# Experts' rows added by token block and transposed at once, with the norm scales applied behind the first projections

## The chip, the cores and the metric

The kernel runs on one core of one Trainium2 chip. The metric is the device time of one execution in microseconds (us). The kernel before took 2353.63 us, the median of 3 runs (2353.54 to 2357.41).

## The reference, cut to what matters

Two transformer stacks follow each other on 512 tokens (T) of width 1024 (D). The change lies where the first ends and the second begins:

```python
h = h + hierarchical_moe(rms_norm(h, norm2_g), ...)    # 32 experts, top 2 of each token
x = rms_norm(h, final_g)                                # "final norm" of the first stack
h = x
u = rmsnorm(h, norm_mix[0])                             # "mixer norm" of the second stack
q, f, i, g = split(u @ w_in)                            # hgrn2_mixer, 8 heads of 128
forget = lb + (1 - lb) * sigmoid(f); key = 1 - forget; query = silu(q)
# chunked recurrence over the tokens from key, query, value i and log(forget), out gated by silu(g)
h = h + (o * silu(g)) @ w_out
```

With s the experts' sum of a token, fg the final gain, a = 1/sqrt(mean(s^2)+eps) and b the same root of the vector a\*fg\*s, the residual is a\*fg\*s and the mixer's input is (a\*b)\*(fg\*g_mix\*s). Both a and a\*b are one number for a token.

## The kernel before, in words

**Engines.** PE (TensorE) makes every product and transpose, DVE (VectorE) and ACT (ScalarE) everything elementwise, POOL (GpSimd) some of it and the indirect DMAs, SP (SyncE) issues the weight loads. Each engine runs its own list in order; semaphores tie the lists together.

**Weights in two parts.** Outside the experts every float32 product is three products of rounded parts (`product`, L527 to L531: hi by hi, lo by hi, hi by lo). A weight unit is 128x2048 (1 MB). SP loads it into one of 4 `raw` slots, ACT rounds it to `w_hi` and DVE subtracts to `w_lo` (`split`, L1154 and L1586). Activations are held as `u_hi`, `u_lo`, 8 chunks (KC) of 128 features by 512 tokens.

**Experts.** 17 rounds of 2 experts each. Every round streams 12 units (`moe_w`, L474, L484) and POOL gathers the tokens' rows (L2288) by a slot table that it read back just before (L2282, L2283); the round's results are scattered to `pair_rows` in DRAM (L2298). Behind the last round POOL waits for that scatter, loads `over_slots` (L2307), asks whether any expert overflowed (not here), and issues the four reads of `y_pairs` (L2326), one for each block of 128 tokens.

**Between the stacks.** DVE adds each token's two expert rows to the residual (L1885, L1887, two 128x1024 operations for each block b), ACT squares each row with its sum (L1309), a root and a reciprocal give the final norm's scale, and DVE multiplies the rows by it (`xn`, L1894). Only then does PE transpose them (L810, 32 transposes), and DVE writes the chunks times fg to `hs` (L1899). The mixer norm follows: ACT squares `hs` (L1325), PE sums by a product with ones (L826), ACT takes the root (L1349), DVE the reciprocal (L1906), and for each chunk DVE scales (`u_tmp`, L1915), ACT rounds (`u_hi`, L1358) and DVE subtracts (`u_lo`, L1910).

**Recurrent stage.** 4 pairs of heads (p), each with 4 weight units j: f (j=0), q (j=1), value (j=2), gate (j=3), each in two halves, so 16 "beats" for a pair. The two halves of unit j use PSUM banks (2j+half)%4. ACT reads the PSUM halves itself: Sigmoid (L1439), Silu (L1441), Copy (L1443), Silu (L1446). `recurrent_work(beat)` on each engine does the recurrence's pieces beside the projections, from beat 11 on: POOL forms exponents (`fx`, L2347, L2348), ACT exponentiates them (L1394), DVE multiplies keys (`k_dec`, L2006), POOL queries (`q_dec`, L2360), PE forms scores of a level (L887), DVE takes them by a mask (L2015). Once for each head come the far scores (operands L1376 to L1381 and L1991 to L1995, PE L865 to L871), the head's output (PE L899, DVE L2023) and its norm (PE L908, ACT L1417, DVE reciprocal L2030 and L2031, `o_lo` L2054). f becomes key and log (L2066, L2067, L1429, scan L2075). The order of all this is written by hand:

```python
for half in range(2):               # PE, unit j of pair p
    ... feature_chunk(..., recurrent_work(beat + 2 * half) after its 4th k)
    mm.then_inc(proj_ready if half == 0 else unit_used, 1)
    recurrent_work(beat + 2 * half + 1)
```

Of the kernel before, what the change touches and what calls it, by code (L numbers as in the profile page):

```python
# [7 lines left out]
ALU = mybir.AluOpType  # L8
# [63 lines left out]
def columns(*sizes):  # L72
    at, out = 0, {}
    for name, n in sizes:
# [8 lines left out]
P2_COLS, P2_N = columns(("n2g", D), ("w_r", KC * 36), ("b_r", 36), ("fg", KC), ("pairs", 4 * TB))  # L83
P3_COLS, P3_N = columns(("n_mix", 2 * KC), ("n_ffn", 2 * KC), ("lb", 3 * KC), ("og", 1), ("levels", 8 * P),
                        ("fin", D), ("cos", T), ("sin", T), ("band", 3 * 256))
P3_FIRST = P3_COLS["fin"][0]
P3_ROOM = (P3_FIRST + 7) // 8 * 8
# [28 lines left out]
def build(nc, x_in, weights_in, constants_in, phase1_in, phase2_in, phase3_in, out):  # L116
    with ExitStack() as ctx:
# [11 lines left out]
        at_a = at_par + (max(P1_N, P2_N, P3_N, P3_ROOM + 6 * T) * 4 + 31) // 32 * 32  # L129
# [96 lines left out]
        y_pairs = place("y_pairs", [TB, 2, D], at_a)  # L226
# [20 lines left out]
        u_tmp = [place(f"u_tmp{n}", [T], at_a2 + (3 + n) * KB2) for n in range(3)]  # L247
# [4 lines left out]
        at_room = at_par + P3_ROOM * 4  # L252
# [14 lines left out]
        lbs = [place(f"lbs{n}", [KC], at_x + 384 + 32 * n) for n in range(6)]  # L267

# [101 lines left out]
        def norm_bank(k):  # L370

            return bank[4 if k else 7]

# [39 lines left out]
        y_landed, y_landed_from = [*y_free, table_written, slots_landed], (160, 144, 144, 64)  # L413
# [7 lines left out]
        n_sq, n_sum, n_root, u_ready = sem("n_sq"), sem("n_sum"), sem("n_root"), sem("u_ready")  # L421
# [26 lines left out]
        def _(sp):  # L448
# [38 lines left out]
            for j in range(RAW):  # L487
                sp.wait_ge(unit_used, U_EXTRA + j + 1)
                sp.dma_start(raw[:, j], weights_in[U_EXTRA + j]).then_inc(raw_landed[j], 16)
            def stream(first, end):  # L490
# [30 lines left out]
        def _(pe):  # L521
# [283 lines left out]
            pe.wait_ge(xn_ready, 2 * TB)  # L805
            for c in range(KC):
                if c >= 4:
                    pe.wait_ge(h0_ready, c - 3)
                for b in range(TB):
                    mm = nc.tensor.transpose(bank[c % 4][:, b * P:b * P + P], xn[:, b, c * P:c * P + P], ident)  # L810
                mm.then_inc(h_turned, 1)

            def norm(k):

                at = norm_bank(k)
                if k:
                    pe.wait_ge(n_acc, 6 * k)
                    nc.tensor.matmul(at[:], ones, sq_acc[:], start=True, stop=False)  # L820
# [104 lines left out]
            for p in range(HH // 2):  # L925
                for j in range(4):
# [5 lines left out]
                    if j == 1 and p:  # L932
                        pe.wait_ge(g_taken, 2 * p)
# [1647 lines left out]
```

## Time and profile before

| | |
|---|---|
| median of 3 runs | 2353.63 us |
| the profiled execution, its own time | 2358.84 us |
| its span in the profile | 2357.0 us |
| mean granted TensorE clock | 0.957 |
| busy PE, DVE, ACT, POOL | 88%, 40%, 28%, 15% of the span |

All starts below are microseconds from the span's start. The span holds the first stack's mixer (to about 310), the router and the experts (to 893), the passage between the stacks (893 to 945), the recurrent stage (945 to 1240) and the rest, which the change leaves alone. A start and a duration belong to one instruction or to merged ones (x8 is eight records).

### The profile page before, as it was taken

The numbers are of one execution on the slowest core, as the hardware profiler recorded it, in microseconds if no ns is written. First come the engines' busy times: TensorE is split into PE (matmuls) and PEld (weight loads), VectorE is DVE, ScalarE is ACT, GpSimd is POOL, SyncE is SP. The second block draws the span as 40 slices with busy tenths as digits, with TensorE's granted clock in tenths as the row PEclk, the third lists the DMA queues.
The fourth block names the chain that finished last, engine by engine and source line by source line (L and its number), as shares of the span: only waits on it lengthen the run. The fifth ranks groups of instructions, "written<-read, shape, count | busy, mean of one in ns | idle before, by whom it ended". The sixth has DMA issues, their size and how long they took to land.

```text
span 2357.0 us, 25197 instructions
## 1 busy us (share of the span) xinstructions
PE 2080.2 (88%) x9900; PEld 1510.4 (64%) x9900; DVE 937.3 (40%) x1125; ACT 669.2 (28%) x835; POOL 352.8 (15%) x349
## 2 busy tenths in 40 slices
PE   6997756877777773999989999999999999999997
PEld 5884532332223221788877888887788987888876
DVE  5428640000000004567765432444775334332333
ACT  3433220000000002666744221223222423221222
POOL 0000002000000000355551110011343201100100
PEclk9997777999999997999999999999999999999999
DMA  5220145999999993211122222223222322222220
GB/s 200 90 90 1 51 193 216 422 421 422 421 421 420 421 420 146 72 63 64 57 76 72 90 106 90 90 91 123 76 86 90 138 77 90 90 95 101 89 90 36
DMA packets 57636, 377.51 MB, mean 160 GB/s; under 512 B 8944, under 2 KB 9040, under 8 KB 14032
## 3 DMA queue, kind: packets, MB, share of 16 engines
q1 hardware_dynamic: 50544, 358.83, 38.8%
q0 software_dynamic: 7008, 17.50, 2.0%
q8 instruction: 61, 1.00, 0.2%
q14 instruction: 23, 0.19, 0.0%
HBM read 370.46 MB, written 15.26 MB: 164 GB/s over the span
## 4 chain that ended last, share of the span: by engine, by line
PE 69%; DMA 18%; DVE 7%; issue 3%; ACT 2%; POOL 1%; SPq 0%; DVEq 0%; POOLq 0%; ACTq 0%
PE bank L529 19%; PE bank L530 19%; PE bank L531 19%; DMA moe_w<-weights_in 17%; PE bank L748 2%; PE bank L725 2%; PE bank L887 2%; PE bank L899 1%; POOL k_rot L2398 1%; DVE w_lo L1586 1%; PE bank L1095 1%; DVE tile L1703 1%; DVE o_tmp L2030 0%; DVE tile L1714 0%; DVE tile L1710 0%
## 5 line engine op out<-in xcount | busy, mean ns | idle before, releaser
L529 PE MATMUL bank<-u_hi,w_hi 128*128 128x512 f32 x1216 | 489.0, 402 | 7.6 <-DVE u_lo L1910 6.4
L530 PE MATMUL bank<-u_lo,w_hi 128*128 128x512 f32 x1216 | 481.3, 396 | 0.0
L531 PE MATMUL bank<-u_hi,w_lo 128*128 128x512 f32 x1216 | 481.0, 396 | 0.0
L1586 DVE TENSOR_TENSOR w_lo<-raw,w_hi 128x2048 fp32r<-128x2048 f32 x96 | 234.1, 2439 | 292.8 <-ACT w_hi L1154 292.6
L725 PE MATMUL bank<-moe_w,xe 128*64 128x512 f32 x1088 | 263.3, 632 | 87.7 <-DMA moe_w<-weights_in 86.5
L529 PEld LDWEIGHTS bank<-u_hi,w_hi 128*128 128x128 f32 x1216 | 228.6, 188 | 66.4 <-issue 10.8
L531 PEld LDWEIGHTS bank<-u_hi,w_lo 128*128 128x128 f32 x1216 | 228.5, 188 | 55.9
L530 PEld LDWEIGHTS bank<-u_lo,w_hi 128*128 128x128 f32 x1216 | 228.9, 188 | 55.2 <-issue 2.2
L1154 ACT ACTIVATE w_hi<-raw 128x2048 fp32r<-128x2048 f32 x96 | 183.6, 1912 | 272.1 <-PE bank L531 271.4
L725 PEld LDWEIGHTS bank<-moe_w,xe 128*64 128x64 f32 x1088 | 91.6, 145 | 258.5 <-issue 258.4
L529 PE MATMUL bank<-w_hi,u_hi 128*128 128x256 f32 (+1 forms) x512 | 155.3, 303 | 12.5 <-DVE u_lo L1721 6.8
L530 PE MATMUL bank<-w_lo,u_hi 128*128 128x256 f32 (+1 forms) x512 | 152.7, 298 | 0.0
L531 PE MATMUL bank<-w_hi,u_lo 128*128 128x256 f32 (+1 forms) x512 | 152.4, 298 | 0.0
L1859 DVE TENSOR_TENSOR hid<-gate,bank 128x512 f32<-128x512 f32 x17 | 11.7, 689 | 339.0 <-PE bank L725 339.0
L2387 POOL TENSOR_TENSOR f_gate<-f_gate,rms 128x512 f32<-128x512 f32 x44 | 57.0, 1296 | 566.5 <-ACT f_gate L1471 566.5
L529 PE MATMUL bank<-hid_hi,w_hi 128*128 128x512 f32 x352 | 139.2, 395 | 0.2
L748 PE MATMUL bank<-moe_w,hid_t 128*64 128x512 f32 x544 | 123.6, 596 | 17.7 <-ACT hid_t L1277 6.4
L530 PE MATMUL bank<-hid_lo,w_hi 128*128 128x512 f32 x352 | 139.0, 395 | 0.0
L531 PE MATMUL bank<-hid_hi,w_lo 128*128 128x512 f32 x352 | 139.0, 395 | 0.0
L2103 DVE TENSOR_TENSOR f_hid<-f_gate,bank 128x512 f32<-128x512 f32 x44 | 30.3, 689 | 212.6 <-PE bank L531 212.6
L529 PEld LDWEIGHTS bank<-w_hi,u_hi 128*128 128x128 f32 x512 | 97.7, 191 | 18.1 <-DVE u_lo L1721 8.3
L530 PEld LDWEIGHTS bank<-w_lo,u_hi 128*128 128x128 f32 x512 | 97.7, 191 | 3.1
(395 smaller groups left out, 2645.5 us busy)
## 6 DMA issues: line engine op xcount, KB each, us to landing
moe_w<-weights_in SPq DMA_DIRECT2D x204, 1024.0 KB, 25.1
raw<-weights_in SPq DMA_DIRECT2D x128, 1024.0 KB, 4.8
y_pairs<-pair_rows POOLq DMA_DIRECT2D x4, 1024.0 KB, 8.2
res<-x_in SPq DMA_DIRECT2D x1, 2048.0 KB, 7.7
token_rows<-xn POOLq DMA_DIRECT2D x1, 2048.0 KB, 7.9
v_rows<-vals SPq DMA_DIRECT2D x2, 1024.0 KB
vals<-v_rows SPq DMA_DIRECT2D x2, 1024.0 KB, 7.5
out<-out_tile SPq DMA_DIRECT2D x4, 512.0 KB, 2.6
```

The costliest lines, as they stand in the source:

```text
L529: nc.tensor.matmul(out_ap, a_hi, b_hi, start=first, stop=False)
L530: nc.tensor.matmul(out_ap, a_hi, b_lo, start=False, stop=False)
L531: return nc.tensor.matmul(out_ap, a_lo, b_hi, start=False, stop=last)
L725: mm = nc.tensor.matmul(bank[2 + j // 2][rows, :], xe[:, c, rows], moe_w[2 * j + b][:, w], start=c == 0, stop=c == KC - 1)
L748: mm = nc.tensor.matmul(bank[5 + half][rows, :], hid_t[:, c, rows], moe_w[2 * j + b][:, w], start=c == 0, stop=c == 3)
L887: mm = nc.tensor.matmul(bank[4 + n % 2][:, t], left, right, start=True, stop=True)
L899: mm = nc.tensor.matmul(bank[6][:, b * P:], val[s][:, b, hh * P:hh * P + P], ws[:, b, 0:T - b * P], start=b == 0, stop=b == TB - 1)
L1095: mm = nc.tensor.matmul(bank[6 + i % 2][:, b * P:b * P + P], vals[:, g, from_block, h * P:h * P + P], flat[:, n * P:n * P + P], start=s == ...
L1154: nc.scalar.activation(w_hi[:, n % 2], raw[:, n % RAW], ACT.Copy).then_inc(hi_ready, 1)
L1586: nc.vector.tensor_tensor(w_lo[:, n % 2], raw[:, n % RAW], w_hi[:, n % 2].bitcast(F32), ALU.subtract) \
L2103: nc.vector.tensor_tensor(f_hid[s][:], f_gate[s][:], bank[2 * s + 1][:], ALU.mult).then_inc(f_prod, 1)
L2387: nc.gpsimd.tensor_tensor(f_gate[n][:], f_gate[n][:], rms[:], ALU.mult).then_inc(f_gated, 1)
```

## The change

The two rows of a token are added as before, but into a buffer of their own (`row_sum`), and PE transposes each block's sum as soon as it is there, unscaled. ACT and DVE make `u_hi` and `u_lo` straight from PSUM with the product of both gains, and ACT copies the residual out. The two per-token scales are worked out from row sums beside the first products; two products with ones spread them over all partitions (`spread_late`), and DVE multiplies each projection by them on its way out of PSUM (`normalize`), the value through ACT's scale. POOL multiplies the residual. The `y_pairs` reads move from POOL's queue to SP's; the `over_slots` load moves ahead of the first gather; the second half of the third parameter block is loaded at the start of the router and the lower-bound arithmetic runs there; the Exp for it too.

```diff
 SP, behind the 4 raw loads of the first units, ahead of the raw stream:
+            sp.wait_ge(pairs_stored, PAIRS_STORED)
+            for b in range(TB):
+                sp.dma_start(y_pairs[b][:], pair_rows[...]).then_inc(y_landed[b], 16)
 PE:
-            pe.wait_ge(xn_ready, 2 * TB)
-            for c in range(KC): ...
-                    mm = nc.tensor.transpose(bank[c % 4][...], xn[:, b, ...], ident)
-            norm(0)
+            for b in range(TB):
+                pe.wait_ge(res2_ready, b + 1)
+                for c in range(KC):
+                    mm = nc.tensor.transpose(bank[c][:, b * P:b * P + P], row_sum[:, b, c * P:c * P + P], ident)
+                    if b == TB - 1:
+                        mm.then_inc(h_turned, 1)
+            def spread_late():
+                pe.wait_ge(hs_out, HS_OUT + KC)
+                for n in range(2):
+                    pe.wait_ge(diag_ready, DIAG_READY + n + 1)
+                    nc.tensor.matmul(bank[6 + n][:], ones, late_diag[n][...], start=True, stop=True).then_inc(n_sum, 1)
                     if j == 1 and p:
-                        pe.wait_ge(g_taken, 2 * p)
+                        pe.wait_ge(pre_ready, PRE_READY + 6 * p)
                     if j == 2:
-                        pe.wait_ge(f_sig, 2 * p + 2)
+                        pe.wait_ge(pre_ready, PRE_READY + 6 * p + 2)
                     if j == 3:
-                        pe.wait_ge(q_taken, 2 * p + 2)
+                        pe.wait_ge(pre_ready, PRE_READY + 6 * p + 4)
                     for half in range(2):
+                        if p == 0 and j < 2:
+                            pe.wait_ge(hs_out, HS_OUT + 2 * j + half + 1)
...
+                        if (p, j, half) == (0, 1, 0):
+                            spread_late()
 ACT:
+            def row_square(b): ... ACT.Square, row_sum -> row_sq, accum late[:, 0]
+            def high(c):     # waits h_turned; u_hi from bank[c], scale mix_gain
+            def residual(c): # waits u_lo; hs from bank[c], scale fg
+            for b in range(TB - 1):
+                row_square(b)
+            for c in range(3):
+                high(c)
+            act.wait_ge(res2_ready, TB)
+            residual(0)
+            for c in range(3, KC):
+                high(c)
+            row_square(TB - 1)
+            residual(1)
+            split(U_HG + 1)
+            for c in range(2, KC):
+                residual(c)
+            ... Sqrt of late[:, 4:6]; split(U_HG + 2)
+            ... late_row[0], late_row[1] copied from bank 6, 7
 ACT, each pair (Sigmoid and Silu now from SBUF, behind DVE):
+                            act.wait_ge(pre_ready, PRE_READY + 6 * p + half + 1)
+                            nc.scalar.activation(run[s][:, half], run[s][:, half], ACT.Sigmoid).then_inc(f_sig, 1)
 DVE:
-            ... reciprocal, xn (L1894), hs (L1899), norm(0)
+            for c in range(KC):
+                dve.wait_ge(u_hi_ready, 2 * KC + c + 1)
+                nc.vector.scalar_tensor_tensor(u_lo[:, c], bank[c][:], mix_gain[:, c:c + 1], u_hi[:, c], mult, subtract)
+            row_squares(0); row_squares(1); split(U_HG + 1); row_squares(2); row_squares(3)
+            ... 3 small operations, reciprocal, late_diag[0], late_diag[1], split(U_HG + 2)
+            def normalize(p, j, tile):
+                for half in range(2):
+                    (waits proj_ready or unit_used)
+                    nc.vector.tensor_tensor(tile[:, half], bank[(2 * j + half) % 4][:], late_row[0][:], ALU.mult) \
+                        .then_inc(pre_ready, 1)
                     recurrent_work(beat + 2)
+                    if j == 0 and p:
+                        normalize(p, 0, run[s])
+                    if j == 1:
+                        if p == 0:
+                            dve.wait_ge(late_ready, LATE_READY + 1)
+                            normalize(0, 0, run[s])
+                        normalize(p, 1, qry[s])
+                    if j == 3:
+                        normalize(p, 3, o_raw[:, 2 * p:2 * p + 2])
                     recurrent_work(beat + 3)
 POOL:
+            pool.dma_start(par3[:, P3_FIRST:], phase3_in[:, P3_FIRST:])   # behind par2's, in the router
             pool.wait_ge(slots_landed, 48)
+            pool.dma_start(over_slots[0:CAP], slot_table[MAIN + P:]...).then_inc(slots_landed, 16)
...
-            pool.dma_start(over_slots ...)      # was here, behind the last scatter
             pool.wait_ge(slots_landed, 64)
             (asks for an overflow)
-            for b in range(TB):
-                pool.dma_start(y_pairs[:, b], ...)
+            nc.gpsimd.memset(y_mark[:], 0).then_inc(pairs_stored, 1)
...
+            pool.wait_ge(late_ready, LATE_READY + 2)
+            for c in range(KC):
+                nc.gpsimd.tensor_tensor(hs[:, c], hs[:, c], late_row[1][:], ALU.mult).then_inc(h0_ready, 1)
```

For p = 0 the Ln, the key arithmetic and the Sigmoid stand one unit later than for the other pairs (Sigmoid in j=1, Ln in j=2). The second parameter block grows by 1024 columns (`fg_row`).

## Rows read from the trace of the kernel before

**Rows 1.** The page, the chain that ended last, shares by engine.
```profile
PE 69%; DMA 18%; DVE 7%; issue 3%; ACT 2%; POOL 1%; SPq 0%; DVEq 0%; POOLq 0%; ACTq 0%
```
**Rows 2.** The chain in order of time, 899 to 943: start, duration, what.
```profile
899.08 3.32 DMA over_slots<-slot_table
...
903.89 5.33 DMA y_pairs<-pair_rows
918.12 1.30 DVE res L1887
...
922.35 2.75 DVE xn L1894 x4
925.14 6.13 PE bank L810 x32
931.27 7.46 PE bank L826 x16
...
939.47 3.37 DVE rms L1906
```
**Rows 3.** Timeline of PE, 945 to 983: units j=0, 1, start of j=2, far scores.
```profile
945.14 0.77 PE L529 MATMUL bank<-u_hi,w_hi 128*128 128x512 f32 x1 [6.43 <-DVE u_lo L1910]
...
951.46 0.47 PE L529 MATMUL bank<-u_hi,w_hi 128*128 128x512 f32 x1
...
954.28 0.40 PE L529 MATMUL bank<-u_hi,w_hi 128*128 128x512 f32 x1
...
971.08 0.28 PE L529 MATMUL bank<-w_hi,u_hi 128*128 128x256 f32 x1
...
982.44 0.38 PE L865 MATMUL bank<-far_q,far_k 128*128 128x128 f32 x2
```
**Rows 4.** The windows: busy time of each engine, granted clock, DMA share, GB/s.
```profile
440.00:880.00 440.00, 341.92 (x1518) 129.15 (x1516) 33.64 (x56) 36.62 (x62) 27.45 (x27) 0.96 1.01 421
943.00:950.00 7.00, 4.86 (x12) 3.42 (x12) 6.96 (x12) 3.67 (x6) 0.00 (x0) 0.56 0.00 0
1081.00:1149.00 68.00, 68.00 (x406) 58.36 (x405) 49.11 (x74) 45.06 (x64) 33.91 (x43) 1.00 0.17 63
```
**Rows 5.** Timeline of POOL where the experts begin; SP's first refill.
```profile
368.72 1.05 POOL L2288 DMA_INDIRECT x_rows<-token_rows,slots  x1 [2.17 <-DMA slots<-slot_table]
...
382.12 83.45 SPq L474 DMA_DIRECT2D moe_w<-weights_in  x40
```
**Rows 6.** Single lines (ns: mean, or minimum/median/maximum), and raw's loads to landing.
```profile
L1325 ACT ACTIVATE sq<-hs 128x512 f32<-128x512 f32 x8 | 5.1, 632 | 10.4 <-DVE hs L1899 5.4 <-PE bank L826 4.9
L2103 DVE TENSOR_TENSOR f_hid<-f_gate,bank x44: 689/689/689, 1292.5 to 2282.4; 128x512 f32<-128x512 f32 x44
L2387 POOL TENSOR_TENSOR f_gate<-f_gate,rms x44: 1282/1297/1297, 1290.3 to 2278.2; 128x512 f32<-128x512 f32 x44
DMA to landing us min/median/max: 4.6/4.8/26.1
```
**Rows 7.** Timeline of ACT and DVE beside pair 2's unit j=1, 1099 to 1108.
```profile
1099.72 0.60 ACT L1441 ACTIVATE qry<-bank 128x512 f32<-128x512 f32 x1 [1.57 <-PE bank L531]
1100.34 1.28 ACT L1394 ACT_TABLE_LOAD   x1
...
1101.54 0.42 DVE L2006 TENSOR_TENSOR k_dec<-fx,key 128x256 f32<-128x256 f32 x1
...
1103.70 1.07 DVE L2006 TENSOR_TENSOR k_dec<-fx,key 128x256 f32<-128x256 f32 x1
```
**Rows 8.** Timeline of PE, POOL and DVE, 1103 to 1142, before two level scores.
```profile
1103.26 1.05 PE L887 MATMUL bank<-q_dec,k_dec 128*128 128x128 f32 x8
...
1106.06 2.66 POOL L2347 TENSOR_TENSOR fx<-run 128x256 f32<-128x256 f32 x1
...
1140.57 0.41 DVE L2006 TENSOR_TENSOR k_dec<-fx,key 128x256 f32<-128x256 f32 x1
...
1141.04 1.16 PE L887 MATMUL bank<-q_dec,k_dec 128*128 128x128 f32 x8
```

More of the change, by code:

```diff
@@ L225, in build @@
         over_slots = tiny("over_slots", [N_OVER, 2], I32)
-        y_pairs = place("y_pairs", [TB, 2, D], at_a)
+        y_pairs = [place(f"y_pairs{b}", [2, D], at_b + 20 * KB2 if b == 3 else at_a + 4 * b * KB2) for b in range(TB)]
         MAIN = P * NPAIR
@@ new lines, in _ @@
+                    if j == 1:
+                        for half in range(2):
+                            act.wait_ge(pre_ready, PRE_READY + 6 * p + half + 3)
+                            nc.scalar.activation(qry[s][:, half], qry[s][:, half], ACT.Silu).then_inc(q_taken, 1)
+                    if j == 2:
+                        for half in range(2):
+                            if half == 0:
+                                act.wait_ge(proj_ready, 4 * p + j + 1)
+                            else:
+                                act.wait_ge(unit_used, n + 1)
+                            for b in range(2):
+                                c = slice(b * 256, b * 256 + 256)
+                                last = nc.scalar.activation(val[s][:, 2 * half + b], bank[half][:, c], ACT.Copy,
+                                                            scale=late[:, 7, 2 * half + b:2 * half + b + 1])
+                            last.then_inc(v_taken, 1)
@@ L1447, in _ @@
+                    if j == 3:
+                        for half in range(2):
+                            act.wait_ge(pre_ready, PRE_READY + 6 * p + half + 5)
+                            nc.scalar.activation(o_raw[:, 2 * p + half], o_raw[:, 2 * p + half], ACT.Silu).then_inc(g_taken, 1)
                     recurrent_work(beat + 3)
@@ new lines, in _ @@
+            chain(nc.vector.tensor_scalar(late[:, 3], late[:, 2], EPS, None, ALU.mult))
+            nc.vector.scalar_tensor_tensor(late[:, 3], late[:, 1], 1.0 / D, late[:, 3], ALU.mult, ALU.add).then_inc(rms_arg, 1)
+            dve.wait_ge(root_ready, 4)
+            chain(nc.vector.reciprocal(late[:, 6:8], late[:, 4:6]))
+            for n in range(2):
+                nc.vector.tensor_tensor(late_diag[n][:], ident.unsqueeze(1).to_broadcast([P, TB, P]),
+                                        late[:, 7 - n].unsqueeze(2).to_broadcast([P, TB, P]), ALU.mult).then_inc(diag_ready, 1)
@@ L1920, in split_trip @@
+            split(U_HG + 2)
             def split_trip(n, i, per):
```

228 lines of the change are left out of this document (107 added, 121 removed).

## The prediction

> **What bounds the kernel now.** I read first the page's chain that ended last: PE holds 69% of it, DMA 18% [rows 1]. The DMA part is the experts' stream: from 440 to 880 the queues move 421 GB/s at a share of 1.01, so nothing but a later start can touch that stretch [rows 4]. Then the same chain in order of time between the stacks [rows 2]. Here the work is a string with one engine busy at a time: the scatter's landing, the `over_slots` load, the reads, DVE's adds, the scaling of the rows, PE's transposes, the squares, a reciprocal. PE makes its first projection product at 945.14, and runs it cold [rows 3]; the granted clock from 943 to 950 is 0.56, near the level of 1.2 GHz, after PE had been idle [rows 4]. Last the windows of the recurrent stage: in 68 us of one pair PE is busy all 68, DVE 49.11, ACT 45.06 [rows 4]. So between the stacks latency counts, and behind them PE counts, as long as DVE's answers come in time.
>
> **The working.** It is made against the profiled execution (2358.84 us), which is 5.2 above the median; the difference found is then taken off the median of 2353.63.
>
> *Term 1, the lookup and the reads.* Before: the scatter has landed at 899.08; `over_slots` takes 3.32, 1.49 pass until the first read is issued at 903.89, and it lands 5.33 later, at 909.22 [rows 2]. After: the 3.32 goes; the question for an overflow stays (1.49); a small memset and a semaphore to SP replace the issue, which no row shows: I take 0.4 (bounds 0.1, and 1.0 from the time of one POOL DMA issue [rows 5]). SP's 1 MB loads land 4.8 after issue, 4.6 at least [rows 6]. First block at 899.08+1.49+0.4+4.8 = 905.8, so **-3.4**. The four reads move past SP's raw load for unit 5 of the stage, which is used tens of us later: nothing. DVE's adds take (919.42-909.22)/4 = 2.55 a block [rows 2], and 1 MB at 421 GB/s takes 2.49 [rows 4], so reads don't fall behind the adds. The adds end at t0 = 919.42-3.4.
>
> *Term 2, `over_slots` ahead of the first gather.* It delays the gather at 368.72 by one POOL issue; behind it wait SP's refills, the first at 382.12 [rows 5], and from there the stream is full. One issue is about 1.0 [rows 5]; its many 8-byte pieces may also hold the queue. Lower bound 0.9, upper the whole 3.32 less the 1.0 already counted [rows 2]. I take **+1.2**. The parameter loads and lower-bound arithmetic moved into the router run beside its PE and DMA pauses and under the experts' first gather: nothing; without that cover some 3 us of DVE.
>
> *Term 3, from the last add to unit j=2.* Before: 971.08-919.42 = 51.66 [rows 2, 3]. After, counted from t0: PE transposes the last block's first chunk, 6.13/32 = 0.19 [rows 2], with its semaphores 0.4. ACT makes three `high`s and `residual(0)`, 0.632 each [rows 6]: 2.9. PE's first product then starts, because it writes bank 0, which `residual(0)` reads. `u_lo` is not in the way: its last chunk is there at about 6.8 (eight `high`s, a `residual`, one DVE operation) and PE is cold: (951.46-945.14)/5 = 1.26 a chunk, later (971.08-954.28)/24 = 0.70 [rows 3]. Four cold and four warm chunks: 2.9+5.0+2.8 = 10.7. `residual(1)` frees bank 1 at about 8. Three more halves of 5.6: 27.5. `spread_late` adds two float32 products of the kind that took 7.46/8 = 0.93 before [rows 2]: **29.4**. Its inputs (row squares, root, reciprocal, two diagonals: some 17 us by DVE's order) are ready before PE stands there at 21.9. The term is 29.4-51.66 = **-22.3**. If PE were still warm from the earlier blocks' transposes it would gain 2.2 more; if cold through the first unit, 6 less.
>
> *Term 4, the late scales in pair 0.* After `spread_late`, ACT has the rows at 24.6; f and q leave PSUM by 30.1, f's arithmetic, split, Ln and scan on DVE and ACT end near 37.5, the far exponents at 38.4, far operands at 40.1. PE asks for them at 29.4+(982.44-971.08) = 40.8 [rows 3]. So 0.7 spare. POOL's 8 multiplies of `hs` at 1.297 [rows 6] fill 24.6 to 35.0 and finish before the scan. Where POOL and DVE run together, rows show single operations stretched: `k_dec` 1.07 for 0.42 [rows 7]. Stretching two or three of them by 0.65 gives 2; minus the spare, I take **+1.5** (bounds 0 and 6).
>
> *Term 5, `normalize` in pairs 1 to 3.* Each adds a 128x512 product out of PSUM, 0.689 [rows 6], between PE and ACT. DVE has the time (49.11+4.1 of 68), but not everywhere the slack:
> - j=0 stands where DVE idles: 0, and ACT comes 0.7 later.
> - j=1 comes behind the reciprocal of the head's norm, at 1101.54. It moves the `k_dec` there by 1.3 and ends it when PE asks, 1103.26 [rows 7, 8]. ACT's second Silu was at 1099.72 [rows 7] and now waits until 1102.9; the exponent behind it, and the next `k_dec`s, come 1 to 2 late where they had 1.5 to 2.4: about 1.0 lost.
> - j=3: the `k_dec` for the next pair starts at 1140.57 and takes 0.41; PE's scores start at 1141.04 [rows 8]. No slack: 1.3 lost.
>
> 2.3 a pair, three pairs: **+7** (bounds 0, and six times two operations of 0.689, 8.3, plus ACT's table load of 1.28 [rows 7] three times, 12).
>
> Sum: -3.4+1.2-22.3+1.5+7 = **-16.0**. Median 2353.6-16.0 = **2337.6**.
>
> **A rule weighed.** POOL's `fx` took 2.66 beside DVE's weight split [rows 8]. The Trainium skill, "SBUF — State Buffer", section "Who interferes with whom", says that a DVE instruction with two SBUF inputs and a GpSimd one that reads SBUF exclude each other for a whole instruction, and that one with at most one SBUF input does not contend. That row agrees. By it `normalize` (one input in PSUM) is free of POOL, while in pair 0 the split and scans alternate with POOL's multiplies, which is rival B.
>
> **The rivals.**
> - *A: the slack holds.* DVE's and ACT's lists shift without holding PE in pairs 1 to 3. For it: DVE idles 19 of 68 us; against it: the 0.06 at 1141. Terms 1 to 4: -23.0, 2330.6. Chance 0.20.
> - *B: pair 0 is held by POOL.* DVE's four key operations, split and two scans each stand behind one multiply of 1.297 [rows 6], 9.1 less 0.7 spare: 8.4 in place of 1.5. For it: the 2.66 [rows 8]; against it: DVE would have to lose at each. -9.1, 2344.5. Chance 0.13.
> - *C: the hand-off decides.* Each of the nine DVE-to-ACT units of pairs 1 to 3 (j=0, 1, 3) puts two products (1.38), an activation (0.60) and a table load (1.28) in PE's way [rows 6, 7]: 3.26 each, 29.3 in place of 7. +6.3, **2359.9**, slower. It decides once a unit costs over 2.6 (23.0/9). For it: DVE and ACT both near 70% and in-order; against it: PE has a whole unit until it needs the bank again. Chance 0.05.
> - *D: little arrives.* Term 2 at its upper end (3.3), PE cold for the whole unit (6 less), B's 8.4 and term 5 at its upper end 12: -3.4+3.3-16.3+8.4+12 = +4.0 at most; its middle, half of these surpluses, -6. Chance 0.07, of it 0.05 within 0.2%.
> - The forecast: 0.55.
>
> **How the numbers follow.** What a measurement here can tell from no change is about 0.2%, 4.7 us. The forecast's own range is 2331 to 2344. The range takes in A and B, with term 1 to 4's bounds at the lower end: 2327 to 2348, leaving out C, most of D and the tails. Faster holds the forecast, A, B and 0.02 of D: 0.90; same 0.05; slower 0.05.
>
> **What would show it.** In the profile after: no `over_slots` between the last scatter and the reads, first add near 907 (with the 1.2); transposes in four groups; first projection product about 3 behind the last add, at about 920, at a low granted clock, four chunks long; PE at unit j=2 near 946 to 947; then gaps of PE in front of the level scores of 1.3 at the start of pairs 1 to 3's following units, released by `k_dec`. SP's first refill near 383.3. Wrong it would be if PE waits before the products for `residual` or `u_lo` beyond 3 us, if `spread_late` waits, if the far scores of pair 0 wait over 2, or if the recurrent stage holds no waits (A) or one in every unit (C).

## The result and the profile after

| | before | after |
|---|---|---|
| median (range) of the runs, us | 2358.09 (2353.54 to 2362.63), 6 runs | 2344.23 (2342.65 to 2347.74), 6 runs |
| ratio, 95% interval | 1 | 0.9946 [0.9931, 0.9962] |
| profiled execution: time, span, mean granted clock | 2358.84, 2357.0, 0.957 | 2347.55, 2345.7, 0.958 |

The kernel became 13.9 us faster by the medians of 6 runs each. Forecast were 16.0 less, 2337.6, from a median of 2353.6 that rested on three runs. The time lies in the range. Part of that is luck: 4.5 us of the 6.6 between 2337.6 and 2344.2 are the old median, which stood that much too low, and so 2344.2 also falls on the number of rival B (2344.5), whose difference of 9.1 did not come.

To see where the time went I use ACT's copies into `w_hi` as milestones: the first behind the experts, the last of the recurrent stage, and the first behind the second attention. Timeline of ACT, the kernel before:

```profile
892.66 1.90 ACT L1154 ACTIVATE w_hi<-raw 128x2048 fp32r<-128x2048 f32 x1
...
1246.77 1.90 ACT L1154 ACTIVATE w_hi<-raw 128x2048 fp32r<-128x2048 f32 x1
...
1911.09 1.92 ACT L1154 ACTIVATE w_hi<-raw 128x2048 fp32r<-128x2048 f32 x1 [8.85 <-PE bank L531]
```

The same three, the changed kernel:

```profile
897.68 1.90 ACT L1176 ACTIVATE w_hi<-raw 128x2048 fp32r<-128x2048 f32 x1
...
1232.18 1.90 ACT L1176 ACTIVATE w_hi<-raw 128x2048 fp32r<-128x2048 f32 x1
...
1899.84 1.92 ACT L1176 ACTIVATE w_hi<-raw 128x2048 fp32r<-128x2048 f32 x1 [8.85 <-PE bank L545]
```

In these rows the brackets hold the engine's idle time before the instruction and what ended it. The three copies cut the execution into a **head** (to 892.66, now 897.68), the change's **own stretch** (354.11 long, now 334.50: -19.6) and a stretch that the change does not touch, FFN and **second attention** (664.32, now 667.66: +3.3). Behind it nothing differs. The spans differ by 11.3: +5.0 - 19.6 + 3.3. So the own stretch gained more than forecast (17.2 without term 2), and the two others gave back 8.3, of which term 2 had 1.2. Most of this study is about those 8.3 and about terms 4 and 5.

The chain that ended last, the changed kernel, shares by engine (beside [rows 1]):

```profile
PE 63%; DMA 18%; DVE 9%; issue 5%; ACT 3%; POOL 1%; SPq 0%; DVEq 0%; POOLq 0%; ACTq 0%
```

The chain in order of time between the stacks, the changed kernel (beside [rows 2]):

```profile
898.75 5.05 DMA pair_rows<-y_rows,slots
903.83 0.50 POOLq L198
...
905.00 4.72 DMA y_pairs<-pair_rows
909.75 1.29 DVE row_sum L1946
...
918.62 1.29 DVE row_sum L1948
919.96 0.49 PE bank L827
920.47 0.69 ACT u_hi L1337
921.19 1.42 DVE u_lo L1952 x2
922.61 0.49 issue
923.10 0.47 PE bank L543
```

The scatter has landed at 903.80, and `over_slots` is gone from behind it. The last add ends at 919.91, and PE's first product starts 3.2 later (before: 25.7 later). The timeline of PE shows how fast it runs there and where unit j=2 starts (beside [rows 3]); its last line is the wait in pair 0:

```profile
923.10 0.47 PE L543 MATMUL bank<-u_hi,w_hi 128*128 128x512 f32 x1 [1.44 <-DVE u_lo L1952]
...
923.86 0.40 PE L543 MATMUL bank<-u_hi,w_hi 128*128 128x512 f32 x1
...
924.57 0.39 PE L543 MATMUL bank<-u_hi,w_hi 128*128 128x512 f32 x1
...
947.28 0.28 PE L543 MATMUL bank<-w_hi,u_hi 128*128 128x256 f32 x1
...
961.63 0.49 PE L876 MATMUL bank<-far_q,far_k 128*128 128x128 f32 x2 [2.84 <-DVE far_q L2034]
```

A chunk of three products takes 0.7, not 1.26: in this execution PE was at its upper level, 2.4 GHz, from about 921.3 on. The windows of the changed kernel (beside [rows 4]) have the granted clock as third column from the end; the third line holds the wait in pair 0, the fourth lies behind it, the fifth is one pair:

```profile
920.00:925.00 5.00, 3.56 (x16) 3.03 (x17) 3.57 (x6) 4.53 (x8) 0.00 (x0) 0.87 0.00 0
925.00:930.00 5.00, 5.00 (x23) 4.00 (x22) 4.93 (x8) 5.00 (x8) 3.06 (x5) 1.00 0.01 3
958.00:962.00 4.00, 1.16 (x10) 0.96 (x9) 3.40 (x7) 3.03 (x9) 3.31 (x6) 1.00 0.48 203
962.00:966.00 4.00, 4.00 (x14) 3.27 (x13) 0.24 (x1) 2.41 (x4) 3.24 (x5) 0.57 0.00 0
1068.00:1136.00 68.00, 67.26 (x397) 57.03 (x396) 51.93 (x80) 43.80 (x64) 35.05 (x42) 1.00 0.18 63
```

PE's wait of 2.84 in pair 0 is followed by 4 us at a granted 0.57, near 1.2 GHz. What held DVE there stands in its and POOL's timelines:

```profile
942.56 10.62 POOL L2395 TENSOR_TENSOR hs<-hs,late_row 128x512 f32<-128x512 f32 x8 [11.94 <-ACT late_row L1362]
...
948.08 1.07 DVE L2116 TENSOR_SCALAR run<-run,lbs,lbs 128x512 f32<-128x512 f32 x1
949.19 1.40 DVE L2117 TENSOR_SCALAR key<-run 128x512 f32<-128x512 f32 x1
950.51 1.52 DVE L2116 TENSOR_SCALAR run<-run,lbs,lbs 128x512 f32<-128x512 f32 x1
952.07 1.40 DVE L2117 TENSOR_SCALAR key<-run 128x512 f32<-128x512 f32 x1
953.39 2.28 DVE L1628 TENSOR_TENSOR w_lo<-raw,w_hi 128x2048 fp32r<-128x2048 f32 x1
```

The four key operations take 5.39 while POOL's 8 multiplies run. The split begins when those are done, and is not stretched.

### The profile page after: what moved, and what is told of

It is laid out like the page before. It is cut to its first block, busy times and chain, and to the rows that moved or that the text cites. A ratio compares the mean times of both kernels' runs of the same rounds, so it can differ in the third digit from the quotient of the medians.

```text
span 2345.7 us, 25203 instructions
## 1 busy us (share of the span) xinstructions
PE 2081.7 (89%) x9888; PEld 1512.2 (64%) x9888; DVE 944.3 (40%) x1142; ACT 669.2 (29%) x843; POOL 367.3 (16%) x354
## 4 chain that ended last, share of the span: by engine, by line
PE 63%; DMA 18%; DVE 9%; issue 5%; ACT 3%; POOL 1%; SPq 0%; DVEq 0%; POOLq 0%; ACTq 0%
PE bank L543 18%; PE bank L544 18%; PE bank L545 18%; DMA moe_w<-weights_in 17%; PE bank L739 3%; PE bank L762 2%; DVE o_tmp L2069 1%; PE bank L660 1%; DVE w_lo L1628 1%; POOL k_rot L2459 1%; PE bank L1117 1%; DVE k_dec L2045 1%; DVE tile L1745 1%; PE bank L898 1%; PE bank L910 1%
```

## The experiments

Twelve runs follow: the two kernels again, and ten variants, each made from the changed kernel unless the table says otherwise. The twelve ran on three chips: the first four together, then turn_end to unscaled, then the last four. The ratio is against the kernel before on the same chip; medians of different chips are compared only roughly. The three stretches are those of the profiled execution.

| kernel | median, us | ratio, 95% interval | head | own stretch | FFN and 2nd attention |
|---|---|---|---|---|---|
| before | 2358.09 | 1 | 892.66 | 354.11 | 664.32 |
| before_again | 2359.72 | 1.0004 [0.9992, 1.0015] | 895.05 | 353.92 | 658.82 |
| lookup_only (of before) | 2356.31 | 0.9992 [0.9982, 1.0003] | 891.62 | 349.64 | 660.45 |
| before_share (of before) | 2352.94 | 0.9978 [0.9968, 0.9988] | 894.93 | 353.67 | 660.41 |
| after | 2344.23 | 0.9946 [0.9931, 0.9962] | 897.68 | 334.50 | 667.66 |
| after_again | 2345.43 | 0.9941 [0.9927, 0.9954] | 892.86 | 334.53 | 667.70 |
| lookup_back | 2348.06 | 0.9954 [0.9940, 0.9967] | 894.05 | 338.44 | 664.50 |
| turn_end | 2347.70 | 0.9950 [0.9934, 0.9966] | 896.33 | 337.36 | 666.48 |
| hs_spread | 2345.60 | 0.9942 [0.9929, 0.9955] | 894.05 | 337.50 | 667.89 |
| norm_late | 2346.90 | 0.9952 [0.9939, 0.9965] | 893.95 | 337.89 | 667.58 |
| unscaled | 2340.53 | 0.9918 [0.9904, 0.9932] | 895.67 | 330.65 | 666.19 |
| hs_dve | 2347.35 | 0.9948 [0.9935, 0.9962] | 895.40 | 337.79 | 666.22 |
| share_wait | 2340.81 | 0.9917 [0.9902, 0.9932] | 894.12 | 337.77 | 660.41 |
| hs_share | 2339.31 | 0.9922 [0.9909, 0.9935] | 892.99 | 334.64 | 660.47 |

**before_again** and **after_again** change nothing.

> The kernel before, unchanged, profiled a second time. The question: in the two profiles at hand the changed kernel lost 4.65 us in the first stack, of which 0.9 can be the earlier over_slots load, and 3.3 us in the second attention's output, where nothing was changed. Theory X (chance: where the clock falls from run to run): this profile differs from the first one of the same kernel by 1 us or more in those same stretches (first stage markers at 322.68, attention output 59.2 us long from 1841.14 to 1900.33). Theory Y (the change shifts these stages for good): this profile has them within 0.5 us of the first. Time ratio 1.000 either way.

> The changed kernel, unchanged, profiled a second time. Theory X (chance): ACT's marker of the first stack that stood at 327.33 in the first profile moves by 1 us or more towards 322.7, and the attention output (62.5 us long from 1826.54 to 1889.08) is again near 59 to 60. Theory Y (systematic): 327.3 and 62.5 again within 0.5. The handover from the experts' last add to unit j=2 should be 27.4 again, and the pair period 69.7, under both. Time about 14 us under before, ratio 0.994.

Theory X holds for the head: it scatters by up to 4.8 within one kernel. Its mean is 893.6 over the four profiles of before's family and 894.7 over the ten of after's, so some 4 of the 5.0 between the two first profiles were chance. In the attention the changed kernel gave 667.66 and 667.70, as theory Y had it, and the kernel before 664.32 and 658.82: one kernel with two values 5.5 apart, as X had it. The own stretch repeats within 0.2 here (354.11, 353.92; 334.50, 334.53), but not always: share_wait below has the changed kernel's code in it and took 337.77. Of these 3.3 more, 2.0 lie in the first unit, where PE was cold, and 1.3 at the end of the stage, where the granted clock was 0.50 for 6.8 us instead of 3.4. So a difference of 3 us between two single profiles of the own stretch proves little by itself; the differences used below are those of places inside it.

Where this comes from is one line of DVE's timeline. The kernel before, first profile (DVE, then POOL):

```profile
1829.95 12.00 DVE L1586 TENSOR_TENSOR w_lo<-raw,w_hi 128x2048 fp32r<-128x2048 f32 x1 [7.48 <-ACT w_hi L1154]
...
1827.47 0.79 POOL L2430 DMA_DIRECT2D share_turned<-share_rows  x1
1828.28 4.08 POOL L2435 TENSOR_TENSOR prob<-prob,share 128x512 f32<-128x512 f32 x4
1832.31 7.48 POOL L2435 TENSOR_TENSOR prob<-prob,share_turned 128x1024 f32<-128x1024 f32 x4
```

The same kernel, second profile:

```profile
1832.13 5.01 DVE L1586 TENSOR_TENSOR w_lo<-raw,w_hi 128x2048 fp32r<-128x2048 f32 x1 [7.48 <-ACT w_hi L1154]
...
1830.11 0.79 POOL L2430 DMA_DIRECT2D share_turned<-share_rows  x1 [0.51 <-DMA share_rows<-share]
1830.91 4.08 POOL L2435 TENSOR_TENSOR prob<-prob,share 128x512 f32<-128x512 f32 x4
1834.94 9.55 POOL L2435 TENSOR_TENSOR prob<-prob,share_turned 128x1024 f32<-128x1024 f32 x4
```

The split is an operation of 2.29. In the first profile it ends at 1841.95, 2.15 behind the last of POOL's multiplies (1839.79): POOL's two groups follow one another without a pause, and DVE gets in nowhere. In the second it ends at 1837.14, and POOL's next group takes 9.55 instead of 7.48, 2.07 more: POOL waited for DVE. POOL had stood 0.51 before it issued the DMA ahead of the first group, because `share_rows` landed late. Eleven profiles have no wait added there. This idle time of POOL is 0.40 and 0.51 in the two with the short split (lookup_only, before_again), and 0 to 0.22 in the nine with the long one. So a few tenths of a microsecond go with 7 us of DVE. With the long split PE stands 2.87 until 1842.05, and its clock falls. The changed kernel has the long form too, with its wait of PE (DVE, then PE):

```profile
1815.35 12.08 DVE L1628 TENSOR_TENSOR w_lo<-raw,w_hi 128x2048 fp32r<-128x2048 f32 x1 [7.48 <-ACT w_hi L1176]
...
1827.53 0.36 PE L543 MATMUL bank<-w_hi,u_hi 128*128 128x256 f32 x1 [2.95 <-issue]
```

**lookup_only** is the kernel before with terms 1 and 2 alone:

```diff
             pool.wait_ge(slots_landed, 48)
+            pool.dma_start(over_slots[0:CAP], slot_table[...]).then_inc(slots_landed, 16)
...
-            pool.dma_start(over_slots[0:CAP], slot_table[...])
...
-            for b in range(TB):
-                pool.dma_start(y_pairs[:, b], ...).then_inc(y_landed[b], 16)
+            nc.gpsimd.memset(y_mark[:], 0).then_inc(rows_set, 1)
...
+            sp.wait_ge(rows_set, 3)
+            for b in range(TB):
+                sp.dma_start(y_pairs[:, b], ...).then_inc(y_landed[b], 16)
```

> The kernel before with the change's terms 1 and 2 alone: over_slots loaded ahead of the first gather, y_pairs read by SP behind a semaphore. The scaling and the turning stay as they were. My steps: scatter's landing to the last add 16.1 instead of 20.3 (-4.2), SP's first refill 0.8 to 0.9 later, together -3.3, about 2354.8 against 2358.1. Rival (the 8-byte pieces of over_slots hold the queue, upper bound of term 2): first refill 2.3 later, together -1.9. Rival (the early load costs the whole 4.6 us seen at the first refill): together +0.4.

From the scatter's landing to the last add it took 16.1, and the own stretch is 4.3 to 4.5 shorter than in the two profiles of before. The head is the shortest of all (891.62), but heads scatter by 4.8, so that alone rules out neither 2.3 nor 4.6. From the slots' first load to the first gather 3.92 pass instead of 3.30, 0.6 more, which is near the step's 0.8 to 0.9. The medians say 3.4 less than before_again, on the same chip, and 2.3 less than the kernel before there; the interval of the ratio still touches 1. The split of the attention took 4.88, the short form.

**lookup_back** is the changed kernel with that one load moved back:

```diff
             pool.wait_ge(slots_landed, 48)
-            pool.dma_start(over_slots[0:CAP], slot_table[...]).then_inc(slots_landed, 16)
...
+            pool.dma_start(over_slots[0:CAP], slot_table[...]).then_inc(slots_landed, 16)
             pool.wait_ge(slots_landed, 64)
```

> The changed kernel with the over_slots load put back behind the last scatter, alone; the reads stay on SP. If the early load costs 0.9 and the late one 3.3 to 3.5, this kernel is 2.5 slower than the changed one (2346.7 against 2344.2), and the scatter-to-last-add passage is 19.4 to 19.6 instead of 16.1. Rival (early load costs its upper bound, 2.3): 1.0 slower. Rival (the load hides beside the question for an overflow): no slower, and up to 0.9 faster.

The median is 2.6 above after_again's; the intervals overlap. From the first milestone to the end of the last add the trace has 25.3 against 22.2: the late load costs 3.1 of path. The whole own stretch is 3.9 longer: 3.0 ahead of the first unit, 2.7 in it, and 1.6 come back in pair 0. In the first unit PE has 0.77 for its first product, because the clock had fallen here; in pair 0 the wait for `far_q` is there, but no fall follows it.

**turn_end** lets all transposes wait for the last sum:

```diff
             for b in range(TB):
-                pe.wait_ge(res2_ready, b + 1)
+                pe.wait_ge(res2_ready, TB)
```

> The changed kernel, except that PE's transposes of the sums wait for the last of the four adds instead of for their own block's. It undoes 'turned at once'. Theory T (PE came warm to the first projection product because the transposes of earlier blocks kept it at work): 24 transposes of 0.19, 4.6 us, now stand behind the last add, and the first four chunks run near 1.26 instead of 0.70, 2.2 us more; the first product starts 7.5 to 8 after the last add instead of 3.2, the granted clock there is near 0.5 to 0.6, and the kernel is 6 to 7 us slower. Rival U (warmth has another cause, or fewer columns are enough): 4.6 slower, and chunks of 0.70 as now. Rival V (PE's transposes of the late block hide in ACT's three copies): 3 or less slower.

The first product starts 7.6 behind the last add, as theory T had it, but it takes 0.47: PE is at the upper level. The granted clock rose while PE made nothing but the 32 transposes. The windows of turn_end:

```profile
915.00:920.00 5.00, 1.22 (x6) 1.25 (x7) 3.60 (x3) 1.15 (x2) 0.00 (x0) 0.50 0.52 220
920.00:925.00 5.00, 4.32 (x28) 4.08 (x26) 0.68 (x2) 1.40 (x3) 0.00 (x0) 0.74 0.00 0
925.00:930.00 5.00, 3.77 (x16) 3.11 (x17) 4.75 (x9) 5.00 (x10) 0.00 (x0) 1.00 0.00 0
```

So T's second half is wrong, and rival U describes the place: 4.4 later, chunks of 0.7. Of these 4.4 the own stretch keeps 2.9; the rest comes back in pair 0, where PE's wait of 2.83 is there as before but no fall of the clock follows it. The ratio is 0.9950 against 0.9941, with intervals that overlap. "Turned at once" is worth 4.4 in the passage and 2 to 3 us in the end, not 7.

**hs_spread** takes POOL's 8 multiplies out of pair 0's block (ACT also waits for the last of them at the square of the sixth head; its idle time there ended with PE, not with POOL):

```diff
-            pool.wait_ge(late_ready, LATE_READY + 2)
-            for c in range(KC):
-                nc.gpsimd.tensor_tensor(hs[:, c], hs[:, c], late_row[1][:], ALU.mult)...
...
+                for c in {16: (0,), 24: (1, 2), 32: (3,), 40: (4, 5), 48: (6,), 56: (7,)}.get(beat, ()):
+                    nc.gpsimd.tensor_tensor(hs[:, c], hs[:, c], late_row[1][:], ALU.mult)...
```

> The changed kernel, except that POOL's 8 multiplies of hs in pair 0 are spread over POOL's later beats of pair 0 instead of standing in one block beside DVE's key operations. Theory B' (part of rival B: POOL's multiplies stretch DVE's tensor_scalar operations, 0.54 to 1.5 and 0.43 to 1.4, by about 3.8 in sum, and the wait they bring makes the clock fall for another 2): DVE's key operations are back at 0.4 to 0.55, the wait of 2.84 for far_q at 961.6 is gone, the granted clock stays at 1.00 there, 4 to 5 us faster (about 2339.5). Rival (the wait comes from the late scales themselves, which reach ACT and DVE late, as my step's spare of 0.7 had it): the wait stays at 1.5 or more, gain under 1.5. Rival (spread multiplies stretch other DVE work, which PE waits for later): the far_q wait goes, the time does not, and new waits of PE stand in pair 0.

DVE's key operations in hs_spread, the multiplies gone from beside them:

```profile
944.71 0.54 DVE L2118 TENSOR_SCALAR run<-run,lbs,lbs 128x512 f32<-128x512 f32 x1
945.29 0.43 DVE L2119 TENSOR_SCALAR key<-run 128x512 f32<-128x512 f32 x1
945.63 0.54 DVE L2118 TENSOR_SCALAR run<-run,lbs,lbs 128x512 f32<-128x512 f32 x1
946.21 0.43 DVE L2119 TENSOR_SCALAR key<-run 128x512 f32<-128x512 f32 x1
```

1.94 instead of 5.39. PE's wait for `far_q` shrinks from 2.84 to 0.22, the clock stays at 1.00, and the milestone at the end of pair 0 comes 97.22 behind the first instead of 101.19: 4.0 gained. Then it is lost again. The beats I had written lie in pairs 1 to 3, not in pair 0, and there the milestones stand 72.3 apart instead of 69.75. The third theory of the text is what happened: PE's waits for `k_dec` behind 1000 grew from 8.1 to 14.5. The ratio is after_again's (0.9942 against 0.9941). hs_dve and hs_share below take the multiplies from POOL too, and their waits for `far_q` are 0.21: three profiles without the multiplies there, three without the wait.

**norm_late** puts the scaling of j=1 and j=3 behind the recurrent work. ACT's Silus move with it (not shown), and the move of j=3 holds in pair 0 too:

```diff
-                    if j == 1:
-                        normalize(p, 1, qry[s])
-                    if j == 3:
-                        normalize(p, 3, o_raw[:, 2 * p:2 * p + 2])
                     recurrent_work(beat + 3)
+                    if j == 1 and p:
+                        normalize(p, 1, qry[s])
+                    if j == 3:
+                        normalize(p, 3, o_raw[:, 2 * p:2 * p + 2])
```

> The changed kernel, except that in pairs 1 to 3 the multiplies by the scale for j=1 and j=3, and ACT's Silu behind them, come after the recurrent work of their beat instead of before it. Theory N (term 5 lives from the two products that stand in front of k_dec and ws on DVE): the pair period falls from 69.75 to 68.1 to 68.5, 4 to 5 us faster. Rival (ACT's work behind them, an exponent and a copy, is what is late): the waits of 0.16 for k_dec and 0.37 for ws stay, no gain within 1 us. Rival (the bank comes free later and PE's next projection unit waits for it): a new wait for proj banks, and slower by 1 to 4.

None of the three as written. The period of a pair grew from 69.75 to 70.67, and the own stretch by 3.4. PE's waits for `k_dec` rose from 8.1 to 11.3, for `ws` they fell from 3.3 to 2.0, and none for a bank came. So to move both out of the way of `k_dec` does not help; which of the two moves costs was not told apart. That the work behind ACT's Silu needs the scaled rows soon is my reading, not tested.

**unscaled** leaves the scaling of f, q and the gate out in pairs 1 to 3. DVE's products go, and ACT reads all three from PSUM; of the edit f's line is shown:

```diff
-                            nc.scalar.activation(run[s][:, half], run[s][:, half], ACT.Sigmoid)...
+                            nc.scalar.activation(run[s][:, half], from_bank(p, 0, half, run[s][:, half]), ACT.Sigmoid)...
```

> The changed kernel, except that pairs 1 to 3 leave out the scaling of f, q and the gate by the token's norm: DVE's two products of each such unit are left out, and ACT reads the PSUM bank itself, as in the kernel before. It measures term 5 by itself. Theory: the pair period goes back from 69.75 to 68.05, 5.1 us faster (about 2339), and PE's waits for k_dec and ws go back to before's. Rival (the period is longer for another reason, the lower granted clock of these stages): the period stays above 69, gain under 2. Rival C (each unit costs 2.6 or more): 20 us or more faster.

The period of a pair is 68.07, so the scaling costs 1.68 a pair, 5.0 for the three. The medians agree: 4.9 under after_again, ratio 0.9918 against 0.9941, though their intervals still overlap by a little. The whole own stretch is 3.9 shorter than after_again's, but unscaled was cold in its first unit; against share_wait, which was cold too, it is 7.1 shorter, part of it because share_wait's clock fell near the end of the stage and that of unscaled did not. Rival C is out by a factor of six by the period, of four by these 7.1. PE's waits in the changed kernel from 1000 to 1230, pairs 1 to 3 and the end of the stage (us in total, times, longest):

```profile
PE bank L898 <- DVE k_dec L2045: 8.1, 9, 2.8
PE bank L910 <- DVE ws L2054: 3.3, 5, 1.4
```

And unscaled:

```profile
PE bank L898 <- DVE k_dec L2055: 7.6, 4, 3.1
PE bank L910 <- DVE ws L2064: 2.2, 2, 1.4
```

The two tables differ by only 1.6, but they hide some: a product's record lasts longer than the 0.12 after which the next normally starts. PE in the changed kernel:

```profile
1028.65 0.28 PE L545 MATMUL bank<-w_hi,u_lo 128*128 128x256 f32 x1
1029.31 2.42 PE L910 MATMUL bank<-ws,val 128*128 128x512 f32 x8 [0.38 <-DVE ws L2054]
```

From start to start 0.65 pass, where unscaled has 0.12: 0.53 lost, and only 0.38 of it stand in brackets. Laid side by side with unscaled in this way, the pair that begins at 998.87 loses 1.1 in front of three groups of products (0.32 and 0.25 before `k_dec`'s at 1020.23 and 1055.44, 0.53 here), and the rest in steps of some 0.1 or less at these and four other such groups. So most of the cost is PE waiting for `k_dec` and `ws` in small pieces.

**hs_dve** gives the 8 multiplies to DVE, in pairs 1 and 2:

```diff
+                if beat == 24:
+                    dve.wait_ge(late_ready, LATE_READY + 2)
+                for c in {24: (0, 1), 26: (2, 3), 40: (4, 5), 42: (6, 7)}.get(beat, ()):
+                    nc.vector.tensor_tensor(hs[:, c], hs[:, c], late_row[1][:], ALU.mult)...
```

> The changed kernel, except that DVE makes the 8 multiplies of hs, two at each of four places in pairs 1 and 2 where it idled 3.2 us, in place of POOL in pair 0. Theory: the spread-out version lost its 4.0 of pair 0 again because POOL's multiplies collide with DVE wherever they stand; on DVE they cost nothing. Expected: PE's wait for far_q stays away, pair 0 ends 4.0 earlier as there, the pair period stays 69.75, so from the first split behind the experts to the last projection of the stage 330.5 instead of 334.5, about 4 us faster than the changed kernel. Rival (the four places are not free: a k_dec or ws behind them comes late): the period of pairs 1 and 2 grows by 1 or more, gain under 2. Rival (clock falls at the stage's end move): the pair periods are as expected, but 1 to 2 us are lost between 1190 and 1230.

The first rival holds. Pair 0 has its gain again (`far_q` waits 0.21), but pairs 1 and 2 are 2.0 and 2.3 longer, in the one unit with the multiplies. PE's timeline in hs_dve:

```profile
1020.56 1.16 PE L898 MATMUL bank<-q_dec,k_dec 128*128 128x128 f32 x8 [0.87 <-DVE k_dec L2045]
...
1026.77 2.42 PE L910 MATMUL bank<-ws,val 128*128 128x512 f32 x8 [1.32 <-DVE ws L2054]
```

0.87 and 1.32 where the changed kernel has none and 0.38. In the own stretch this comes out even: hs_share, the same code there and warm as after is, took 334.64 for 334.50. (The 337.79 of hs_dve is a cold first unit, as share_wait's 337.77 is.) The beats chosen lie one unit ahead of the places where DVE idles 3.2; those places (beats 28, 30, 44 and 46, as I read the trace) were not tried.

**share_wait** adds one wait of POOL in the second attention, behind which DVE can get in; **before_share** is the same line in the kernel before, **hs_share** joins it with hs_dve:

```diff
                 if i == 2 * AH:
                     pool.wait_ge(order_landed, LANDED_FROM + 32)
+                    pool.wait_ge(lo_ready, nth(U_QKV + 15) + 1)
```

> The changed kernel with one wait more in a stage that the change does not touch: in the second attention POOL waits for DVE's split of the fourth value unit before it starts its last four multiplies. Theory S (a race of two engines decides 5.5 us there: DVE's split of 2.29 us took 12.0 to 12.15 in eight profiles, in which POOL's multiplies followed one another without a pause, and 5.01 in the second profile of the kernel before, where POOL paused for a DMA): the split takes 5.0, PE's stall of 2.95 and the wait for vals behind it are gone, the stretch from the end of the recurrent stage to the end of the attention shrinks by 5 to 9, the kernel is 5 to 9 us faster than the changed one (2335 to 2340). Rival (the fall of the clock is the cause, and the long split only its companion): the split is short and the kernel gains under 2. Rival (PE waits for the probabilities that POOL now gives 2.3 later): a new wait, gain under 3.

> The kernel before with the same wait of POOL in the second attention. Theory S: without the wait this kernel lost the race in one profile of three (its own two and that of the lookup change alone), the changed kernel in all seven of its family. So the wait gives the kernel before about 2 us (a third of 5.5), it stands near 2356.5, its runs scatter less than the 13 us of now, and the changed kernel with the wait is faster than it by 18 to 20 us, the whole of what its own stretch gained (19.5), against 13.9 without. Rival (the changed kernel's loss behind its own stretch is systematic for another reason): the difference of the two kernels with the wait stays near 14.

> The changed kernel with both: DVE's multiplies of hs in pairs 1 and 2, and POOL's wait in the second attention. Theory: the gains add, 4 + 5 to 9, so 9 to 13 under the changed kernel, 2331 to 2335, ratio to before 0.988 to 0.990. Rival (they share the time): no more than the larger of the two alone, 2335 to 2340.

POOL in share_wait now pauses where DVE needs it:

```profile
1813.27 4.07 POOL L2497 TENSOR_TENSOR prob<-prob,share 128x512 f32<-128x512 f32 x4
1819.65 7.50 POOL L2497 TENSOR_TENSOR prob<-prob,share_turned 128x1024 f32<-128x1024 f32 x4 [2.31 <-DVE w_lo L1628]
```

DVE's split took 4.50, PE's stall of 2.95 is gone, and the stretch is 660.41, 7.3 shorter; in before_share it is 660.41 as well. Theory S is shown for the mechanism: one wait gives the changed kernel 4.6 by the medians (2340.81 against 2345.43, on another chip; ratios 0.9917 against 0.9941, their intervals just overlapping) and the kernel before, on the same chip, 6.2 (2352.94 against 2359.16; by the ratio 5.2, interval 2.8 to 7.5). Its count is refuted: if the kernel before lost the race only in one execution of three, it would have gained 2. Three profiles were too few to tell. With the wait the two kernels stand 12.1 apart by the medians, 14 by the ratios, not 18 to 20. The rival "stays near 14" has the number right and the reason wrong: behind the own stretch the two kernels now take the same 660.41, so no loss of the changed one is left there. What is smaller is the gain of the own stretch itself, 15.9 between these two profiles (353.67 and 337.77) instead of 19.5, because PE was cold. hs_share is as fast as share_wait within the intervals. Both beat the kernel before by 0.8%; share_wait is one line.

## Why the prediction was right, and where its steps were off

The forecast of 16.0 less met 13.9, with the sign, the mechanism and the place of most terms right. By its own steps:

- **Term 1, -3.4:** measured -4.2 to -4.5. From the scatter's landing to the last add 20.3 became 16.1. SP's reads were issued 1.20 behind the landing instead of 1.49 + 0.4, and landed 4.72 later.
- **Term 2, +1.2:** the load is on the path with its issue, 0.82, at 372.09, as the lower bound had it; from the slots' first load to the first gather 4.06 instead of 3.30, +0.8. The heads are too scattered (4.8) to show it: the ten profiles with the early load have a mean of 894.5, the four with the late one (before, before_again, before_share, lookup_back) 894.2. The first refill came at 386.76 instead of the 383.3 that was to show it, by the chance of the head (381.95 in after_again).
- **Term 3, -22.3:** from the last add to unit j=2 27.37 instead of 51.66, -24.3. The steps held (3.2 to the first product for 2.9 forecast, no wait at `spread_late`), but PE was not cold; the text had named this case and priced it at 2.2. Whether it is cold is chance. Nine profiles turn the blocks at once. The first product takes 0.47 in five of them (after, after_again, hs_spread, norm_late, hs_share) and 0.76 or 0.77 in four (lookup_back, unscaled, hs_dve, share_wait), whose first unit is some 2.0 longer. In these the term is the -22.3 of the forecast.
- **Term 4, +1.5, mis-sized:** the cover of the split and the scans was right, the stretch was not. hs_spread measures POOL's multiplies at 4.0. The four key operations were stretched by 3.45, not "two or three of them by 0.65", and the wait of 2.84 drew a fall of the clock behind it, which no step had. With the 0.2 left at `far_q` the term is 4.2. Rival B had POOL in the right place and the wrong victims: it counted split and scans, which came after POOL's last multiply. The rule quoted from the Trainium skill, "SBUF — State Buffer", "Who interferes with whom", frees operations with at most one SBUF input, but only outside the modes that use two ports, a condition I left out; the same section lists `tensor_scalar` among those that can run in such a mode. The four key operations are `tensor_scalar`s with one SBUF input, and took up to 1.52 for 0.54.
- **Term 5, +7:** measured 5.0 by the periods, 1.68 a pair for 2.3 (7.1 by the own stretch of unscaled against share_wait, with a fall of the clock in it). That DVE's slack does not hold everywhere was right, so rival A fell. But it did not break in two places by 1.0 and 1.3: the losses are 0.5 and less, in front of seven groups of products.
- **Rival D** took 3.3 for term 2, whose own upper bound is 3.32 less 1.0; its most is +3.0 and not +4.0. Nothing hangs on it.
- **What no step had:** the own stretch sums to -19.6 against -17.2 forecast (all terms but the second). The rest is outside. The second attention has a race between POOL and DVE that a few tenths of a microsecond decide. Both kernels lost it in the two first profiles, and the changed one was still 3.3 longer there. It had a second fall of the clock near 1883, and its first one came not with PE's stall but 8.5 later, at 1836.03, behind a wait of 2.19 for `vals` that is 0.87 in the kernel before. Neither belongs to the change: lookup_only and before_share, made from the kernel before, have the second fall too, and lookup_back, made from the changed one, has neither and took 664.50 for before's 664.32. Why the clock falls there in one execution and not in the other is open.

An estimate from these parts: -19.6 for the own stretch, or -16.3 where the first unit is cold as in share_wait, + 0.8 for the gather, and 0 (lookup_back) to + 3.3 for the attention make -18.8 to -12.2. The runs show 13.9. So the parts are right and of the right size, but that the sum came within 2.1 is partly luck: term 4 came out 2.7 worse, terms 1, 3 and 5 together 4.9 better, and the attention, which no step had, took 3.3 of the gain in the two first profiles.

## What to carry to other kernels

A gain in a latency-bound passage arrives almost whole, but a tuned kernel has races in it that small shifts decide, whatever was changed. Profile both kernels more than once, cut them at the same milestones, and look for single instructions whose duration differs before you credit or blame the change. Where POOL runs a long series of instructions beside DVE, try a wait of POOL at the point where DVE must get in; here it was worth some 5 us. And count what a moved operation does to its new neighbours: the 8 multiplies of `hs` cost 4.0 beside the keys, 4.3 on DVE in pairs 1 and 2, and 7.6 spread over pairs 1 to 3 on POOL.

## What the runs showed of the hardware

- **DVE can be kept out by a whole series of POOL's instructions, not by one.** The split of 2.29 took 11.90 to 12.15 in nine profiles, to the end of up to seven multiplies of POOL that followed one another. It took 4.45 to 5.01 in the other five, where DVE got in between POOL's two groups: in three POOL paused for the added wait, in before_again and lookup_only the first multiply of the second group took 3.9 instead of 1.9. The Trainium skill, "SBUF — State Buffer", "Who interferes with whom", says that a DVE instruction with two SBUF inputs contends with a GpSimd one that reads SBUF. The trace agrees, and the loss was not one multiply of 1.87 but up to 9.8.
- **The clock can fall after short waits too.** The wait of 2.84 for `far_q` in pair 0 stands in seven profiles. In five of them the granted clock fell to 0.50 within 1.4 us behind it, for 3.4 us; in lookup_back and turn_end it did not. The last wait for `k_dec` in the recurrent stage, 2.83 long, stands in all fourteen, and a fall followed it in five. So the cost of a wait of this length is its own, or its own and 1.6 more (pair 0 of after against that of lookup_back), and which of them can differ between executions of one kernel.
- **The clock can rise while PE makes nothing but transposes.** In turn_end the granted clock went from 0.50 to 1.00 during 32 transposes in a row. With eight transposes a block, in four groups, PE was at the upper level for its first product in five profiles of nine, and at the lower in four.
